# A DeltaNet scan on one core: the triangle's inverse by quarter-array products

## The chip, the core and the metric

The kernel runs on one core of a Trainium2 chip. TensorE multiplies (a 128x128 array), VectorE and ScalarE move and change data between PSUM and SBUF, GpSimd does element work in SBUF, SyncE starts transfers. The metric is device time in microseconds; lower is better.

## The reference, cut to what matters

Two layers of a backbone over 512 latent tokens and 256 context tokens, width 1024. Each layer has two SwiGLU blocks and between them a token mixer of four gated DeltaNet heads and eight RWKV-7 heads, each scanned in both directions. The change is in the DeltaNet part:

```python
a_strict = jnp.where(strict, jnp.einsum('bhnid,bhnjd->bhnij', k, k) * decay * beta[..., :, None], 0.0)
rhs = jnp.concatenate([k * (beta * jnp.exp(gc))[..., None], v * beta[..., None]], axis=-1)
sol = lax.linalg.triangular_solve(a_strict, rhs, left_side=True, lower=True, unit_diagonal=True)
...
v_new = u_n - jnp.einsum('bhcd,bhde->bhce', w_n, s)
o_n = jnp.einsum('bhcd,bhde->bhce', qd_n, s) + jnp.einsum('bhij,bhje->bhie', attn_n, v_new)
s = s * cd_n[..., None, None] + jnp.einsum('bhcd,bhce->bhde', kd_n, v_new)
```

Per chunk and head the unit lower triangle I + A is solved. The kernel uses chunks of 128 tokens, so A is 128x128.

## The kernel before, in words

Each engine runs its own program; semaphores order them. A layer has ten phases with all engines waiting at their ends: feed-forward, projection, DeltaNet scan (`pe_dn`, `act_dn`, `dve_dn`, `pool_dn`), projection, features, RWKV scan (`pe_rw` and its relatives), and output and feed-forward phases.

The DeltaNet scan has 6 steps a layer (2 context chunks, then 4 latent ones), 12 in all. Each step handles 8 triangles: four heads in each of two directions (`g` = 0 and 1). Direction g owns PSUM banks 4g to 4g+3 and its own SBUF tiles, four heads side by side. Every engine goes through the steps in a hardware loop (`Fori`).

A step: TensorE spreads the decays (L1279), multiplies keys by keys and keys by queries (L1283, L1288) and transposes (L1292, L1300). VectorE and ScalarE make the decay matrices, GpSimd weights them (L1248, L1251, L1254), VectorE makes A (L1414) and the first X (L1417, L1419). Then the inverse X of I + A is built by doubling: at level l, diagonal blocks of 2^l are inverted, and each pair is joined through the block below its diagonal. Seven levels, 0 to 6, reach 128. Y is X transposed. A level l > 0 is

- `times_even` (L1169): A's transpose times the even column blocks of X, four products of 64 columns a direction;
- a mask on VectorE (L1427, tile TD);
- `times_packed` (L1174): Y times TD;
- a subtraction into X on VectorE (L1431);
- four transposes of X (L1331), which ScalarE copies to Y (L1389).

All products are float32 with 128x128 weights; the two directions alternate, so that one's products cover the other's VectorE work. Level 0 has only the transposes, followed by keys times state (L1338; VectorE uses it in L1437 and L1441). After level 6, Y multiplies the right side (L1345), and the state and output products follow (L1353, L1356, L1357). A float32 product appears in the trace as two records, a transpose as one.

The RWKV scan inverts its triangles in the same manner with chunks of 64. Two 64x64 triangles lie one above the other in 128 partitions, and each product is issued twice, for partitions 0 to 63 and for 64 to 127 (`times`, L1896; `lower_times_x`, L1988; `x_times_lower`, L2001), with VectorE's L2133 and L2143 and ScalarE's L2071. Its TensorE code is unrolled; VectorE, ScalarE and GpSimd loop. In its start VectorE copies the masks it needs (L2104, L2106).

At the very start GpSimd makes the constant masks, `level` among them (L276 to L286); TensorE waits for them (L295).

Of the kernel before, what the change touches and what calls it, by code (L numbers as in the profile page):

```python
# [7 lines left out]
ALU = mybir.AluOpType  # L8
ACT = mybir.ActivationFunctionType

P = 128
# [24 lines left out]
def build(nc, x, c, ctx, c_ctx, ada_w, ada_b, norm_g, ffn_w13, ffn_w2, w_in, dn_conv, dn_a_log, dn_dt_bias,  # L36
# [3 lines left out]
    with es:  # L40
# [69 lines left out]
        level = sb("level", [P, 7, P])  # L110
# [121 lines left out]
        def pool_setup(pool):  # L232
# [44 lines left out]
            for l in range(7):  # L277
                w = 1 << l
                v = level[:, l, :].rearrange("p (b s j) -> p b s j", s=2, j=w)[:, :, 0, :]
                nb = P // (2 * w)  # L280
                then(g.memset(v, 1.0))

                then(g.affine_select(out=v, in_=v, compare_op=ALU.is_ge, fill=0.0, base=-w,
                                     pattern=[[-2 * w, nb], [0, w]], channel_multiplier=1))

                then(g.affine_select(out=v, in_=v, compare_op=ALU.is_ge, fill=0.0, base=2 * w - 1,  # L286
                                     pattern=[[2 * w, nb], [0, w]], channel_multiplier=-1))
# [857 lines left out]
        EVEN = P // 2  # L1145
# [10 lines left out]
        def packed_bank(b, l):  # L1156
            return packed(PS[:, b, 0:4 * EVEN], l)

        def packed_sbuf(t, l):
            return packed(t.rearrange("p a b -> p (a b)")[:, 0:4 * EVEN], l)  # L1160
# [5 lines left out]
        def times_even(pe, b, lhs, x, l):  # L1166

            for u in range(4):
                mm = pe.matmul(packed_bank(b, l)[:, u], lhs[:, u, :], even(x[:, u, :], l, "p"), start=True, stop=True)  # L1169
            return mm  # L1170

        def times_packed(pe, b, lhs, x):
            for u in range(4):
                mm = pe.matmul(PS[:, b, u * EVEN:(u + 1) * EVEN], lhs[:, u, :],  # L1174
                               x.rearrange("p a b -> p (a b)")[:, u * EVEN:(u + 1) * EVEN], start=True, stop=True)
            return mm

# [3 lines left out]
        XS = 6 * LEVELS_DN + RW_CHUNKS * LEVELS_RW  # L1181
        TS = XS - STEPS
        XTS = XS - RW_CHUNKS
# [19 lines left out]
        kst_ready, s_scaled = dsem("kst_ready"), dsem("s_scaled")  # L1203

# [67 lines left out]
        def pe_dn(pe, layer):  # L1272
            for first, steps, a, w in dn_loops(layer):
                with pe.Fori(0, steps) as i:
# [35 lines left out]
                    for l in range(n):  # L1310
# [14 lines left out]
                        for g in range(2):  # L1325
# [4 lines left out]
                            for u in range(DN_H):  # L1330
                                mm = pe.transpose(PS[:, c, u * P:(u + 1) * P], X[g][:, u, :], ident[:, :])  # L1331
# [1228 lines left out]
```

## Time and profile before

| | us |
|---|---|
| median of 3 runs (4900.68 to 4907.02) | 4905.58 |
| profiled execution | 4901.45 |
| its span | 4899.8 |
| TensorE busy in the span | 4409.8 (90%) |
| VectorE | 1991.6 (41%) |
| ScalarE | 1366.0 (28%) |
| GpSimd | 532.2 (11%) |

The rest of the profiled execution lies around the span. The two DeltaNet scans stand at about 874 to 1202 us and 3406 to 3736 us of the span, the two RWKV scans at about 1494 to 1863 and 4023 to 4391. Busy records of TensorE overlap one another, so the distance from one start to the next says more than a record's length. "PEclk" is the granted clock as a share of 2.4 GHz.

### The profile page before, as it was taken

To read this page: it belongs to the slowest core of one execution; us is meant where nothing else is said; L and a number is where in the kernel's file an instruction comes from. 1 tells how busy PE (TensorE), PEld (TensorE's weight loads), DVE (VectorE), ACT (ScalarE), POOL (GpSimd) and SP (SyncE) were. 2 spreads that over 40 slices of the span, in tenths; PEclk is the share of its full clock that TensorE was granted. 3 is DMA by queue.
4 is the path that set the end of the run, shared out by engine and by line. 5 is a ranking of instruction groups with operands and counts; after the bars stand their busy time and mean duration, and the time that the engine had idled before them with its cause. 6 is when DMAs were issued, how large, how long until landed. Compare 5 with 4: busy or idle time off the path is not lost. (4 is left out here: it accounts for less than half of the span.)

```text
span 4899.8 us, 101076 instructions
## 1 busy us (share of the span) xinstructions
PE 4409.8 (90%) x43461; PEld 3932.3 (80%) x43461; DVE 1991.6 (41%) x2817; ACT 1366.0 (28%) x1958; POOL 532.2 (11%) x690
## 2 busy tenths in 40 slices
PE   6999989898948996999998999988998849996998
PEld 5998977887827995889897999977887629984887
DVE  3222254454475445322223222353444484446334
ACT  3211133232242222321113211243222242223322
POOL 1000000332032110000100000001321051100000
PEclk8999999999959998999999999999999859998999
DMA  5233231000200002233423222121000100012332
GB/s 199 79 111 109 71 112 39 14 1 4 60 7 3 4 4 78 78 124 95 154 77 112 66 62 60 59 62 35 1 0 24 47 1 4 4 42 75 97 94 69
DMA packets 344215, 286.50 MB, mean 58 GB/s; under 512 B 9086, under 2 KB 316772, under 8 KB 343396
## 3 DMA queue, kind: packets, MB, share of 16 engines
q1 hardware_dynamic: 326628, 218.92, 15.0%
q0 software_dynamic: 17280, 62.92, 3.7%
q8 instruction: 262, 4.29, 0.4%
q14 instruction: 45, 0.37, 0.0%
HBM read 270.27 MB, written 11.53 MB: 58 GB/s over the span
## 5 line engine op out<-in xcount | busy, mean ns | idle before, releaser
L646 PE MATMUL PS<-x_hi,w_hi 128*128 128x384 f32 (+1 forms) x2464 | 678.1, 344 | 17.6 <-DVE x_lo L550 16.1
L646 PE MATMUL PS<-x_lo,w_hi 128*128 128x384 f32 (+1 forms) x2464 | 676.3, 344 | 0.0
L646 PE MATMUL PS<-x_hi,w_lo 128*128 128x384 f32 (+1 forms) x2464 | 676.2, 343 | 0.0
L646 PEld LDWEIGHTS PS<-x_hi,w_hi 128*128 128x128 f32 x2464 | 450.3, 189 | 38.7 <-issue 24.4
L646 PEld LDWEIGHTS PS<-x_lo,w_hi 128*128 128x128 f32 x2464 | 450.2, 189 | 13.9
L646 PEld LDWEIGHTS PS<-x_hi,w_lo 128*128 128x128 f32 x2464 | 449.7, 189 | 13.7
L779 DVE TENSOR_TENSOR silu_buf<-silu_buf,PS 128x768 f32<-128x768 f32 (+1 forms) x88 | 78.1, 887 | 786.2 <-ACT silu_buf L712 786.2
L1896 PE MATMUL PS<-arena 64*64 64x64 f32 (+1 forms) x9216 | 356.9, 229 | 12.1 <-POOL arena L1879 5.6
L622 DVE TENSOR_TENSOR w_lo<-raw_w,w_hi 128x2048 fp32r<-128x2048 f32 x136 | 311.7, 2292 | 133.2 <-ACT w_hi L617 133.2
L690 PE MATMUL PS<-hidden_hi,w_hi 128*128 128x256 f32 (+1 forms) x1232 | 346.7, 351 | 19.3 <-DVE hidden_lo L784 19.3
L617 ACT ACTIVATE w_hi<-raw_w 128x2048 fp32r<-128x2048 f32 x136 | 259.5, 1908 | 338.5 <-PE PS L690 331.4
L1896 PEld LDWEIGHTS PS<-arena 64*64 64x64 f32 x9216 | 331.4, 136 | 23.1 <-issue 16.6
L690 PE MATMUL PS<-hidden_lo,w_hi 128*128 128x256 f32 (+1 forms) x1232 | 339.3, 345 | 0.0
L690 PE MATMUL PS<-hidden_hi,w_lo 128*128 128x256 f32 (+1 forms) x1232 | 338.5, 345 | 0.0
L690 PEld LDWEIGHTS PS<-hidden_hi,w_hi 128*128 128x128 f32 x1232 | 227.7, 189 | 75.0 <-issue 25.9
L765 DVE SCALAR_TENSOR_TENSOR arena<-PS,mod,arena 128x512 f32 (+3 forms) x168 | 100.2, 632 | 455.3 <-PE PS L690 455.2
L712 ACT ACTIVATE silu_buf<-PS 128x768 f32<-128x768 f32 (+1 forms) x88 | 66.9, 760 | 778.6 <-PE PS L646 778.5
L690 PEld LDWEIGHTS PS<-hidden_lo,w_hi 128*128 128x128 f32 x1232 | 233.2, 189 | 29.7
L690 PEld LDWEIGHTS PS<-hidden_hi,w_lo 128*128 128x128 f32 x1232 | 233.2, 189 | 29.3
L410 POOL DMA_DIRECT2D arena<-in_ada_w_dram x120 | 86.6, 724 | 1340.6 <-PE PS L419 1105.8
L1389 ACT ACTIVATE arena<-PS 128x512 f32<-128x512 f32 x168 | 100.3, 597 | 317.1 <-PE PS L1331 313.4
L2071 ACT ACTIVATE arena<-PS 128x256 f32<-128x256 f32 x240 | 91.8, 383 | 318.9 <-PE PS L1896 316.9
(341 smaller groups left out, 7803.5 us busy)
## 6 DMA issues: line engine op xcount, KB each, us to landing
raw_w<-in_ffn_w_dram SPq DMA_DIRECT2D x240, 512.0 KB, 4.4
arena<-in_ada_w_dram POOLq DMA_DIRECT2D x120, 512.0 KB, 6.1
arena<-in_w_in_dram SPq DMA_DIRECT2D x64, 512.0 KB, 3.9
arena<-in_ada_w_dram SPq DMA_DIRECT2D x6, 2048.0 KB, 14.6
raw_w<-in_ffn_w_dram SPq DMA_DIRECT2D x32, 384.0 KB, 3.5
arena<-in_w_out_dram SPq DMA_DIRECT2D x16, 512.0 KB, 4.2
h_save<-arena SPq DMA_DIRECT2D x16, 384.0 KB, 2.3
arena<-h_save SPq DMA_DIRECT2D x2, 3072.0 KB, 9.9
```

Of the source, the lines that this page charges most:

```text
L410: pool.dma_start(ada_buf[b], src[:, 2 * b:2 * b + 2, bass.ds((first + 4 * i) * P, 4 * P)]).then_inc(ada_landed[b], 16)
L617: nc.scalar.activation(w_split[HI][:, b, :], raw_w[:, b], ACT.Copy).then_inc(w_high_ready, 1)
L622: nc.vector.tensor_tensor(w_split[LO][:, b, :], raw_w[:, b], w_split[HI][:, b, :].bitcast(F32), ALU.subtract).then_inc(w_low_ready, 1)
L646: mm = pe.matmul(PS[:, 4 * b + 2 * g + s, 0:half], w[wo][:, k, g, :], x_split[xo][:, k, a + s * half:a + (s + 1) * half], start=(k == 0 an ...
L690: mm = pe.matmul(PS[:, 2 * c + s, 0:wd], w[wo][:, f, c * P:(c + 1) * P], hid_split[xo][:, f, a0:a0 + wd], start=(f == 0 and q == 0), stop= ...
L712: nc.scalar.activation(silu_buf[:, b, a:T].rearrange("p (s w) -> p s w", s=pieces), PS[:, 4 * b:4 * b + pieces, 0:half], ACT.Silu).then_in ...
L765: ins = nc.vector.scalar_tensor_tensor(v, PS[:, 2 * c + s, 0:w], g, v, ALU.mult, ALU.add)
L779: nc.vector.tensor_tensor(prod.rearrange("p (s w) -> p s w", s=pieces), prod.rearrange("p (s w) -> p s w", s=pieces), PS[:, 4 * b + 2:4 * ...
L1389: sc.activation(Y[g], bank(4 * g), ACT.Copy).then_inc(y_ready[g], 1)
L1896: mm = pe.matmul(PS[p, bank_, at + u * width:at + (u + 1) * width], lhs(u)[p], rhs(u)[p], start=True, stop=True)
L2071: sc.activation(YR[r][g], half_bank(4 * g + 1), ACT.Copy).then_inc(y_ready[g], 1)
```

## The change

The 128x128 triangle is taken apart as two 64x64 triangles on its diagonal and one 64x64 corner below. Levels 0 to 5 never join anything across the middle, so X, Y and the masked product live in packed tiles (`XP`, `YP`, `TP`): partitions 0 to 63 hold the upper block, 64 to 127 the lower one, 64 columns a head. Each product becomes two, one per half of the partitions; transposes become products with a 64x64 identity (`id_c`). The last copies of Y go into the two diagonal blocks of the full tile, and level 6 is done for the corner alone: A's corner times X's upper block, times minus one (`T6`), times the lower block of Y, copied into Y's upper right block. The lower left block of Y is zeroed once a layer. TensorE's loop over the steps is unrolled. The masks are made for 64 columns in both halves by GpSimd at the start, and the RWKV scan uses them in place of its own copies.

```diff
-        level = sb("level", [P, 7, P])
+        level = sb("level", [P, 6, P // 2])
+        id_c = sb("id_c", [P, P // 2])
+        HALVES = (slice(0, 64), slice(64, 128))
...
+            for p in HALVES:
+                then(g.tensor_copy(id_c[p], ident[p, p]))
+                for l in range(6):
+                    w = 1 << l
+                    v = level[p, l, :].rearrange("p (b s j) -> p b s j", s=2, j=w)[:, :, 0, :]
+                    nb = P // (4 * w)
+                    then(g.memset(v, 1.0))
+
+                    then(g.affine_select(out=v, in_=v, compare_op=ALU.is_ge, fill=0.0, base=-w,
+                                         pattern=[[-2 * w, nb], [0, w]], channel_multiplier=1))
+
+                    then(g.affine_select(out=v, in_=v, compare_op=ALU.is_ge, fill=0.0, base=2 * w - 1,
+                                         pattern=[[2 * w, nb], [0, w]], channel_multiplier=-1))
...
+        XP, T6 = ([X[g].rearrange("p a b -> p (a b)")[:, 256 * n:256 * n + 256].rearrange("p (u t) -> p u t", u=DN_H)
+                   for g in range(2)] for n in range(2))
+        TP = [TD[g].rearrange("p a b -> p (a b)")[:, 0:128].rearrange("p (u t) -> p u t", u=DN_H) for g in range(2)]
+        YP = [TD[g].rearrange("p a b -> p (a b)")[:, 256:512].rearrange("p (u t) -> p u t", u=DN_H) for g in range(2)]
...
+        def blocks(b, p=slice(0, P)):
+            return PS[p, b, 0:256].rearrange("p (u t) -> p u t", u=DN_H)
...
         def pe_dn(pe, layer):
+
+            def times(b, width, lhs, rhs):
+
+                for u in range(DN_H):
+                    for p in HALVES:
+                        mm = pe.matmul(PS[p, b, u * width:(u + 1) * width], lhs(u, p), rhs(u, p), start=True, stop=True)
+                return mm
+
             for first, steps, a, w in dn_loops(layer):
-                with pe.Fori(0, steps) as i:
+                for i in range(steps):
...
-                                times_even(pe, c + 1, AT[g], X[g], l).then_inc(tx_summed[g], 1)
+                                for u in range(DN_H):
+                                    for p in HALVES:
+                                        mm = pe.matmul(packed(PS[p, c + 1, 0:128], l)[:, u], AT[g][p, u, p],
+                                                       even(XP[g][p, u, :], l, "p"), start=True, stop=True)
...
-                                times_packed(pe, c + 2, Y[g], TD[g]).then_inc(xd_summed[g], 1)
+                                times(c + 2, 32, lambda u, p: YP[g][p, u, :], lambda u, p: TP[g][p, u, :]).then_inc(xd_summed[g], 1)
...
-                            for u in range(DN_H):
-                                mm = pe.transpose(PS[:, c, u * P:(u + 1) * P], X[g][:, u, :], ident[:, :])
-                            mm.then_inc(x_turned[g], 1)
+                            times(c, 64, lambda u, p: XP[g][p, u, :], lambda u, p: id_c[p]).then_inc(x_turned[g], 1)
...
+                    lo, hi = HALVES
+                    for g in range(2):
+                        for u in range(DN_H):
+                            mm = pe.matmul(blocks(4 * g + 1, hi)[:, u], AT[g][lo, u, hi], XP[g][lo, u, :], start=True, stop=True)
+                        mm.then_inc(tx_summed[g], 1)
+                    for g in range(2):
+                        pe.wait_ge(tx_masked[g], ts + n)
+                        pe.wait_ge(y_ready[g], yt + n)
+                        for u in range(DN_H):
+                            mm = pe.matmul(blocks(4 * g + 2, lo)[:, u], T6[g][hi, u, :], Y[g][hi, u, hi], start=True, stop=True)
+                        mm.then_inc(xd_summed[g], 1)
                     for g in range(2):
                         c = 4 * g
-                        pe.wait_ge(y_ready[g], XTS * layer + n * (first + i) + n)
+                        pe.wait_ge(y_ready[g], yt + n + 1)
                         pe.wait_ge(r_ready[g], it + 1)
                         for u in range(DN_H):
...
-                            sc.activation(Y[g], bank(4 * g), ACT.Copy).then_inc(y_ready[g], 1)
+                                act.wait_ge(xd_summed[g], TS * layer + n * (first + i) + l)
+                            if l < n - 1:
+                                ins = sc.activation(YP[g], blocks(4 * g), ACT.Copy)
+                            else:
+                                for p in HALVES:
+                                    ins = sc.activation(Y[g][p, :, p], blocks(4 * g, p), ACT.Copy)
+                            ins.then_inc(y_ready[g], 1)
+                    lo, hi = HALVES
+                    for g in range(2):
+                        act.wait_ge(xd_summed[g], TS * layer + n * (first + i) + n)
...
+            for g in range(2):
+                v.memset(Y[g][HALVES[1], :, HALVES[0]], 0.0).then_inc(y_ready[g], 1)
...
-                        v.tensor_tensor(X[g], DM[g], bc(level[:, 0, :], 1, [P, DN_H, P]), ALU.mult).then_inc(x0_step[g], 1)
+                        for p in HALVES:
+                            ins = v.tensor_tensor(XP[g][p], DM[g][p, :, p], bc(level[p, 0, :], 1, [P // 2, DN_H, P // 2]), ALU.mult)
+                        ins.then_inc(x0_step[g], 1)
                         dve.wait_ge(x0_step[g], it + 1)
-                        v.tensor_tensor(X[g], bc(ident[:, :], 1, [P, DN_H, P]), X[g], ALU.subtract).then_inc(x_ready[g], 1)
...
-                            dve.wait_ge(tx_summed[g], TS * layer + (n - 1) * (first + i) + l)
-                            v.tensor_tensor(packed_sbuf(TD[g], l), packed_bank(4 * g + 1, l), level_mask(l), ALU.mult).then_inc(tx_masked[g], 1)
+                            dve.wait_ge(tx_summed[g], TS * layer + n * (first + i) + l)
+                            v.tensor_tensor(TP[g].rearrange("p u (b j) -> p u b j", j=1 << l), packed(PS[:, 4 * g + 1, 0:128], l),
+                                            level_mask(l), ALU.mult).then_inc(tx_masked[g], 1)
                         for g in range(2):
-                            dve.wait_ge(xd_summed[g], TS * layer + (n - 1) * (first + i) + l)
+                            dve.wait_ge(xd_summed[g], TS * layer + n * (first + i) + l)
                             dve.wait_ge(x_turned[g], XTS * layer + n * (first + i) + l)
-                            v.tensor_tensor(even(X[g], l), even(X[g], l), packed_bank(4 * g + 2, l), ALU.subtract).then_inc(x_ready[g], 1)
+                            x = even(XP[g], l)
...
+                    for g in range(2):
+                        hi = HALVES[1]
+                        dve.wait_ge(tx_summed[g], TS * layer + n * (first + i) + n)
+                        v.tensor_scalar(T6[g][hi], blocks(4 * g + 1, hi), -1.0, None, ALU.mult).then_inc(tx_masked[g], 1)
...
-                v.tensor_copy(id_c[p], ident[p, p])
                 v.tensor_copy(ak_mask[p, 0:D], upto_strict[p, p])
-                v.tensor_copy(level_c[p], level[p, 1:LEVELS_RW, p])
```

On TensorE, a level before (in the loop's body, here level 1, the turning after it and the start of level 2):

```order
L1169 MATMUL PS<-arena 128x64 x8
L1320 ISA
L1174 MATMUL PS<-arena 128x64 x8
L1327 REGISTER_ALU
L1331 MATMUL PS<-ident,arena 128x128 x8
L1169 MATMUL PS<-arena 128x64 x8
```

The same place in the unrolled code of after (L1323 is A times X, L1273 the helper `times` for Y times TP and for the turning by `id_c`):

```order
L1323 MATMUL PS<-arena 64x32 x16
L1273 MATMUL PS<-arena 64x32 x16
L1273 MATMUL PS<-id_c,arena 64x64 x16
L1323 MATMUL PS<-arena 64x32 x16
L1273 MATMUL PS<-arena 64x32 x16
```

Each set of 8 whole-array instructions has become 16 on quarters of the array, and the register instructions between them are gone.

TensorE at the end of a step before: level 6, the last turning, and the right side L1345:

```order
L1327 REGISTER_ALU
L1331 MATMUL PS<-ident,arena 128x128 x8
L1169 MATMUL PS<-arena 128x64 x8
L1320 REGISTER_ALU
L1174 MATMUL PS<-arena 128x64 x8
L1327 REGISTER_ALU
L1331 MATMUL PS<-ident,arena 128x128 x8
L1345 MATMUL PS<-arena 128x128 x8
```

After: level 5 with its turning, the corner (L1349 is A times X, L1355 is Y times T6), and the right side L1362:

```order
L1323 MATMUL PS<-arena 64x32 x16
L1273 MATMUL PS<-arena 64x32 x16
L1273 MATMUL PS<-id_c,arena 64x64 x16
L1349 MATMUL PS<-arena 64x64 x8
L1355 MATMUL PS<-arena 64x64 x8
L1362 MATMUL PS<-arena 128x128 x8
```

Of level 6 two sets of 8 quarter products are left, without a turning.

VectorE in the head of a step before, where A (L1414) and the first X (L1417, L1419) are made, direction by direction, then the attention product (L1423) and the first mask:

```order
L1414 TENSOR_TENSOR arena<-arena,PS 128x512
L1417 TENSOR_TENSOR arena<-arena,level 128x512
L1419 TENSOR_TENSOR arena<-ident,arena 128x512
L1414 TENSOR_TENSOR arena<-arena,PS 128x512
L1417 TENSOR_TENSOR arena<-arena,level 128x512
L1419 TENSOR_TENSOR arena<-ident,arena 128x512
L1421 REGISTER_ALU
L1423 TENSOR_TENSOR arena<-arena,PS 128x512 x2
L1426 ISA
L1427 TENSOR_TENSOR arena<-PS,level 128x256 x2
```

After (L1442 is A, L1446 and L1449 the first X, L1453 the attention product, L1457 the mask):

```order
L1442 TENSOR_TENSOR arena<-arena,PS 128x512
L1446 TENSOR_TENSOR arena<-arena,level 64x256 x2
L1449 TENSOR_TENSOR arena<-id_c,arena 128x256
L1442 TENSOR_TENSOR arena<-arena,PS 128x512
L1446 TENSOR_TENSOR arena<-arena,level 64x256 x2
L1449 TENSOR_TENSOR arena<-id_c,arena 128x256
L1451 REGISTER_ALU
L1453 TENSOR_TENSOR arena<-arena,PS 128x512 x2
L1456 ISA
L1457 TENSOR_TENSOR arena<-PS,level 128x128 x2
```

Each direction's X comes from three smaller operations in place of two large ones, in the same place of the order.

## Rows read from the trace of the kernel before

**Rows 1.** The page, part 4: chain by line, share of the span.

```profile
PE PS L646 12%; PE PS L832 7%; PE PS L690 6%; PE PS L1896 3%; PE PS L1174 1%; PE PS L1169 1%; PE PS L2001 1%; PE PS L1988 1%; PE PS L1331 1%; PE PS L1338 0%; DVE arena L2220 0%; DVE arena L1793 0%; PE PS L841 0%; PE PS L853 0%; DVE arena L1431 0%
```

**Rows 2.** Stages; columns: window, us, busy per engine (count), clock, DMA.

```profile
874.00:1184.00 310.00, 279.98 (x2180) 258.88 (x2180) 150.68 (x272) 91.87 (x161) 107.28 (x108) 0.93 0.01 3
...
1494.00:1863.00 369.00, 360.50 (x11136) 354.54 (x11136) 150.27 (x441) 96.40 (x240) 41.43 (x118) 0.99 0.02 4
```

**Rows 3.** Chain, end of one DeltaNet step; columns: start us, us, what, count.

```profile
3503.24 0.43 DVE arena L1431
...
3503.71 0.66 PE PS L1331 x4
3504.37 1.73 PE PS L1169 x16
3506.10 1.80 PE PS L1174 x16
...
3507.93 0.43 DVE arena L1431
...
3508.40 0.66 PE PS L1331 x4
...
3509.10 2.05 PE PS L1345 x16
```

**Rows 4.** Chain, last RWKV level of a chunk, same columns.

```profile
4262.08 0.91 PE PS L1988 x32
4262.99 1.05 PE PS L2001 x32
...
4264.05 1.15 PE PS L1896 x32
```

**Rows 5.** Timeline, head of a step; columns: start, us, engine, line, what, idle before.

```profile
3524.93 0.69 DVE L1417 TENSOR_TENSOR arena<-arena,level 128x512 f32<-128x512 f32 x1
...
3525.50 1.04 POOL L1248 TENSOR_TENSOR arena<-arena 128x512 f32<-128x512 f32 x1 [1.33 <-ACT arena L1376]
3525.65 1.44 DVE L1419 TENSOR_TENSOR arena<-ident,arena 128x512 f32<-128x512 f32 x1
...
3528.07 1.59 POOL L1254 TENSOR_TENSOR arena<-arena,upto_incl 128x512 f32<-128x512 f32 x1
...
3528.58 1.64 DVE L1419 TENSOR_TENSOR arena<-ident,arena 128x512 f32<-128x512 f32 x1
...
3530.27 1.12 PE L1331 MATMUL PS<-ident,arena 128*128 128x128 f32 x4 [1.35 <-DVE arena L1419]
...
3531.18 3.62 PE L1338 MATMUL PS<-arena 128*128 128x128 f32 x16
3531.20 1.27 POOL L1254 TENSOR_TENSOR arena<-arena,upto_incl 128x512 f32<-128x512 f32 x1
```

**Rows 6.** Lines; columns: count, ns min/median/max, first and last start, forms.

```profile
L1427 DVE TENSOR_TENSOR arena<-PS,level x144: 423/424/425, 895.3 to 3723.9; 128x256 f32<-128x256 f32 x144
L2133 DVE TENSOR_TENSOR arena<-PS,arena x240: 275/291/293, 1500.8 to 4384.7; 128x128 f32<-128x128 f32 x120
L2071 ACT ACTIVATE arena<-PS x240: 378/383/385, 1503.8 to 4386.8; 128x256 f32<-128x256 f32 x120
L2106 DVE COPY arena<-level x4: 471/474/477, 1492.7 to 4026.4; 64x320 f32<-64x320 f32 x4
```

**Rows 7.** The same for one line of whole-array products.

```profile
L1356 PE MATMUL PS<-arena x192: 274/275/276, 925.5 to 3733.8; 128*128 128x128 f32 x192
```

**Rows 8.** Stretches in the head of the step, columns as in rows 2.

```profile
3532.00:3534.00 2.00, 2.00 (x12) 2.00 (x11) 0.69 (x1) 0.02 (x1) 2.00 (x3) 0.50 0.00 0
```

**Rows 9.** Timeline of the start, columns as in rows 5.

```profile
16.81 1.04 PE L295 MATMUL PS<-ident,arena 113*128 113x113 f32 x4 [16.81 <-POOLq L288]
...
20.76 8.30 PE L307 MATMUL PS<-ident,arena 128*128 128x128 f32 x48 [2.69 <-DMA arena<-in_x_dram]
...
54.44 3.27 PE L385 MATMUL PS<-arena,cs 128*2 128x512 f32 x16 [2.60 <-DMA arena<-in_ada_w_dram]
```

More of the change, by code:

```diff
@@ L1164, in level_mask @@
             return bc(m, 1, [P, 4, m.shape[1], m.shape[2]])
[L1166 to L1176, printed above, removed]
         STEPS = 6 + RW_CHUNKS
-        XS = 6 * LEVELS_DN + RW_CHUNKS * LEVELS_RW
-        TS = XS - STEPS
-        XTS = XS - RW_CHUNKS
+        XS = 6 * (LEVELS_DN - 1) + RW_CHUNKS * LEVELS_RW
+        TS = XTS = XS - RW_CHUNKS
+        Y_MORE = 7
         def dsem(name):
@@ L1203, in build, with y_count @@
         kst_ready, s_scaled = dsem("kst_ready"), dsem("s_scaled")
+        def y_count(layer, c):
+            return (XTS + Y_MORE) * layer + 1 + LEVELS_DN * c
         def dn_loops(layer):
@@ L1308, in pe_dn @@
                         mm.then_inc(at_turned[g], 1)
-                    n = LEVELS_DN
+                    n = LEVELS_DN - 1
+                    xs, ts, yt = XS * layer + n * (first + i), TS * layer + n * (first + i), y_count(layer, first + i)
                     for l in range(n):
@@ L1364, in act_dn @@
             sc = nc.scalar
[L1365 removed]
+            n = LEVELS_DN - 1
             for first, steps, a, w in dn_loops(layer):
@@ L1387, in act_dn @@
                             if l > 0:
-                                act.wait_ge(xd_summed[g], TS * layer + (n - 1) * (first + i) + l)
-                            sc.activation(Y[g], bank(4 * g), ACT.Copy).then_inc(y_ready[g], 1)
+                                act.wait_ge(xd_summed[g], TS * layer + n * (first + i) + l)
[8 more added lines that the diff above has]
+                        act.wait_ge(xd_summed[g], TS * layer + n * (first + i) + n)
+                        sc.activation(Y[g][lo, :, hi], blocks(4 * g + 2, lo), ACT.Copy).then_inc(y_ready[g], 1)
                     for g in range(2):
@@ L1835, in build @@
         ab_mask, ak_mask = region(26880, 2 * D), region(27008, 2 * D)
-        lower0, lower0_t, id_c = (region(27136 + 64 * n, D) for n in range(3))
-        level_c = region(27328, LEVELS_RW - 1, D)
+        lower0, lower0_t = (region(27136 + 64 * n, D) for n in range(2))
+        level_c = level[:, 1:LEVELS_RW, :]
         y_moved, masks_made = dsem("y_moved"), sem("masks_made")
@@ L1849, in rw_counts @@
             own = RW_CHUNKS * layer + c
-            xs = XS * layer + 6 * LEVELS_DN + LEVELS_RW * c
+            xs = XS * layer + 6 * (LEVELS_DN - 1) + LEVELS_RW * c
             ts = TS * layer + 6 * (LEVELS_DN - 1) + (LEVELS_RW - 1) * c
-            xt = XTS * layer + 6 * LEVELS_DN + (LEVELS_RW - 1) * c
+            xt = ts
             return it, own, xs, ts, xt
@@ L1927, in new_values @@
                         pe.wait_ge(r_ready[g], it + 1)
-                        pe.wait_ge(y_ready[g], xt + n - 1)
+                        pe.wait_ge(y_ready[g], xt + Y_MORE * (layer + 1) + n - 1)
                         times(4 * g + 3, 0, D, lambda u: y[g][:, u, :], lambda u: R_T[g][:, u, :]).then_inc(vn_summed[g], 1)
@@ L1997, in x_times_lower @@
                         else:
-                            pe.wait_ge(y_ready[g], xt2 + l - 1)
+                            pe.wait_ge(y_ready[g], xt2 + Y_MORE * (layer + 1) + l - 1)
                         for u in range(NB):
```

33 lines of the change are left out of this document (10 added, 23 removed).

## The prediction

> **What bounds the kernel now.** The page's chain comes first: TensorE holds it nearly throughout, and the DeltaNet scan (lines 1169 to 1345) has some 3% of the span in it [rows 1]. The change is worth what that scan gives. The stretches come next: in the DeltaNet stretch TensorE is busy 280 of 310 us at a mean clock of 0.93, in the RWKV stretch 360 of 369 us at 0.99, with five times as many instructions [rows 2]. The RWKV scan already inverts its triangle with pairs of 64x64 products, so it is the nearest measured relative of what the DeltaNet scan becomes.
>
> Then the chain inside one level. A level is: turn X (L1331), A times X (L1169), mask on VectorE, Y times that (L1174), subtract on VectorE (L1431). The chain runs 0.43 us of L1431, 0.04 of handing over, 0.66 of turning the second direction, 1.73, 1.80, and again L1431: from 3503.71 to 3508.40 it is 4.69 us a level [rows 3]. Only the subtraction of the second direction shows; the masks (0.42 us, rows 6) and ScalarE's copies of Y lie under the other direction's products. The whole-array products set the pace: 16 records in 1.73 us, 0.108 us a record, for only 64 columns. L1345 with 128 columns takes 2.05 us for its 16, a wait included [rows 3], so fewer columns have bought little here, and what a smaller weight block buys is the question.
>
> In RWKV's last level, which has no other work filled in, the same three sets of 32 records take 0.91 (L1988), 1.05 (L2001) and 1.15 us (L1896), 3.11 together, with masks, subtractions and waits in it [rows 4]. That is 0.028 us a record without a wait.
>
> **The sum, for one of 12 steps** (144 masks in L1427 are 12 steps of 6 levels and 2 directions, rows 6).
>
> Levels 1 to 5. Each now has 16 + 16 products of 32 columns and 16 of 64, 96 records, exactly the counts, tiles and columns of rows 4, and the VectorE operations halve from 128x256 to 128x128, 0.42 to 0.29 us, ScalarE's copy from 128x512 to the 0.38 us of 128x256 [rows 6]. So 3.11 in place of 4.69: 1.58 each, 7.9 us. In level 2 the two 128x512 operations L1437, which stand between subtraction and mask, now outlast the products above them: subtraction ends 0.46 after the last product, two L1437 at 0.64 (0.69 for a 128x512 operation alone, rows 5) take 1.28, so the mask starts at 1.74, while the product it reads ends at 1.49 + 0.2. I lose 0.1.
>
> Last level. Before, from the last product of level 5 to L1345: one whole level 4.69, then 0.03 + 0.43 + 0.04 + 0.66 + 0.04, 5.9 us. After, counted from the first turning product (0.05 after that last product, its X being ready): turning 1.15; corner A times X, 8 records a direction on one quarter of the array. Rows of before have no such run. From below they cannot beat 0.028 a record; from above they cost a whole-array record, 0.108. I take 0.057, since each quarter of a pair gets every second record, so each quarter by itself goes at 0.057. First direction 1.15 to 1.61, second to 2.07. VectorE's T6 (64x256 out of PSUM, priced at the 0.42 of L1427) 1.80 to 2.22 and 2.27 to 2.69. ScalarE's two half copies of Y per direction, 0.38 each, end at 1.4 and 2.2, in time. Corner Y times T6: 2.27 to 2.73, 2.73 to 3.2. ScalarE copies the first corner 2.9 to 3.3. VectorE's L1441, queued behind the second T6, ends at 3.39 (0.69 for 128x512, rows 5) and is later, so L1345 starts at 3.45 + 0.05 = 3.5, 2.4 earlier. Its 2.05 us, in which it waits for ScalarE's second copy, become the 1.78 of 16 records. Together 2.65.
>
> Level 0. X is now made by two 64x256 operations and one 128x256 per direction in place of two of 128x512. Undisturbed that is an estimated 1.1 us (three operations between 0.29 and 0.42) for 1.4, twice. But GpSimd works beside it, and the two engines hold each other up: L1417 takes 0.69 alone, L1419 takes 1.44 and 1.64 when it meets L1248 and L1254, and L1254 takes 1.27 or 1.59 [rows 5]. A shorter operation saves only its own length; three can meet three GpSimd operations where two met two. Ends: if none meets, VectorE is done 1.3 us earlier; if the second half product and the subtraction each wait out a GpSimd operation, 0.7 later. I take 0.2 earlier. The second turning has 16 records at half clock (0.96) for 1.12: another 0.15. The slow clock stays: the engine stands at 0.50 after its idle time before L1331, through L1338 (3.62 us for 16 records) and into level 1 [rows 5, 8]; that loss is in both versions. The attention product waits for L1254 of the second direction, which ends 3532.47 [rows 5]; the first product that needs it comes some 2 us later even after the gain.
>
> Between whole-array and quarter products TensorE may have to run empty. No row shows it; it costs from 0 to what a record is longer than its slot, 0.275 less 0.108 [rows 7], 0.17. Two such places lie on the path (into L1338 and out of it), 0.1 each: 0.2. The Trainium skill ("TensorEngine Tiling (Array Packing)", Key Properties) says that a change of tiling mode drains the engine; the scan would then pay the upper end, 0.15 us a step more, and no run yet shows it.
>
> Sum: 7.9 - 0.1 + 2.65 + 0.2 + 0.15 - 0.2 = 10.6 us a step, 127.2 for 12.
>
> Outside. The RWKV stage loses four small copies on VectorE (two of them 0.47 us, rows 6) once a layer; GpSimd's own copies and TensorE's products beside them leave 0.2 a layer, 0.4 in all (0 to 1.2). Setup grows: GpSimd makes the masks for two halves, 38 small instructions for 21, which I make 4 to 5 us longer; TensorE starts L295 at 16.8 right behind it and would reach L307 some 1.5 us late, since that waited 2.69 for the tokens [rows 9]. Later TensorE waits for weights by DMA again, 2.60 us before L385 at 54.4, which swallows it. Cost 0, at most 1.5. The two memsets of Y lie under VectorE's idle time. The unrolled TensorE code is cheap if code arrives in time: RWKV's is unrolled too and is busy 360 of 369 us [rows 2].
>
> The profiled execution took 4901.45 us (span 4899.8), 4 us under the median 4905.58. 4901.5 - 127.6 = 4773.9; against the median 4778.
>
> **Rivals.** (1) The corner does not overlap. If on one quarter a weight load must wait for the product before it, a record costs up to 0.108 and each of the four corner sets 0.86 in place of 0.46. A times X ends 2.87, Y times T6 of the first direction 3.7, its copy 4.3: L1345 starts 0.8 to 1.2 later, 12 to 15 us in all, about 4792. For it: nothing in the trace has this shape. Against: whole-array records share all rows and still start every 0.108 while each lasts 0.275 with its load beside it [rows 7]. The Trainium skill ("TensorE: Matmul & The Clock Gate", The mechanism) says that weight loads overlap running products only where the row group differs; read strictly it gives this rival, and the whole-array records disagree with the strict reading.
>
> (2) GpSimd takes back more at level 0: 0.7 later in place of 0.2 earlier, 0.9 a step, 11 us: 4789. For it the 1.44 and 1.64 of L1419; against it that the new operations are half as long.
>
> (3) Slower than before: the quarter products do not bring the clock back. Each step begins with the engine at 0.50; if it stayed there, a level would take 96 records at 0.057, 5.5 us, 2.4 more than forecast, 12 for five levels, the corner 2 more, and the 64 records from L1345 on, 7 us now, some 6.5 more: 20 us a step against a gain of 10.6, so 10 us a step slower, 5020 to 5030. It decides from half of that work at half clock on. Against it: RWKV's stretch of the same products is at 0.99. For it: only that DeltaNet's steps have an idle time each, which RWKV's have not.
>
> (4) The head gets off lightly: the operations miss GpSimd's, or the clock does not fall since the idle time shrinks: 13 to 20 us better, 4762.
>
> (5) It does not do what it says: code for the unrolled loop arrives late, or quarter pairs do not run side by side. Rows 2 and 4 speak against both.
>
> **Numbers.** Forecast 0.62; rival 1 0.13; rival 2 0.11; rival 4 0.09; rival 3 0.03; rival 5 0.02, near no change or a little slower. Time 4778. Range 4757 to 4806: the low end is the head without GpSimd and free switches of tiling (15 us), with 6 for the forecast's own slack; the high end rivals 1 and 2 together. A measurement of this kernel tells 0.2% (10 us) from no change; faster 0.95, within it 0.01, slower 0.04.
>
> **What would show it.** Levels 2 to 5 at 3.1 us and 0.03 us a record (if 4 or more, the pairs or the hand-overs fail); L1437 the only late VectorE operation; the corner's records 0.057 or 0.108 apart; L1441 or the corner copy releasing the product behind it; the two VectorE operations that make X under L1248, L1251 and L1254; the clock at 0.50 for one stretch a step and 1.00 from level 2 on. I am wrong if the step shrinks by under 8.5 or over 12.5 us, or if something outside the scan moves by more than 3 us.

## The result and the profile after

| | before | after |
|---|---|---|
| median | 4904.1 of 4 runs (4900.68 to 4907.02) | 4781.1 of 4 runs (4776.6 to 4782.66) |
| profiled execution, span | 4901.45, 4899.8 | 4781.18, 4779.5 |
| TensorE busy | 4409.8 | 4290.5 |
| instructions in the trace | 101076 | 107933 |

The ratio is 0.9748 [0.9731, 0.9765]: 2.5% faster, 123 us. The forecast was 4778.

The same stretches as in [rows 2] (DeltaNet, then RWKV; columns as there):

```profile
873.00:1142.00 269.00, 235.70 (x4104) 218.03 (x4104) 140.19 (x284) 83.61 (x181) 102.73 (x108) 0.91 0.02 5
1434.00:1800.00 366.00, 358.33 (x11129) 354.06 (x11131) 149.20 (x438) 95.60 (x239) 42.00 (x119) 0.99 0.02 4
```

From its first product to its last a DeltaNet scan takes 268.3 and 268.1 us in place of 326.8 and 327.0. So 117 of the span's 120 us are in the two scans. Inside them, as the mean of the ten steps that follow another one (worked out from the records; a step is counted from the previous one's last scaling of the state):

| piece of a step | before | after | change | forecast |
|---|---|---|---|---|
| head: until the second direction's first X is made | 13.62 | 14.36 | +0.74 | -0.2 |
| turning, keys times state, to level 1 | 4.36 | 4.81 | +0.45 | +0.05 |
| levels 1 to 5 | 23.92 | 15.49 | -8.43 | -7.8 |
| corner in place of level 6, then right side, state and outputs | 12.40 | 9.73 | -2.67 | -2.65 |
| step | 54.31 | 44.40 | -9.91 | -10.6 |

The levels first. Level 1 begins at the half clock and takes 3.37 us in the mean, 5.16 before; levels 2 to 5 take 3.03 each, 4.69 before. The chain of waits of after, over two of them (columns as in [rows 3]):

```profile
3376.31 2.12 PE PS L1273 x64
3378.43 0.91 PE PS L1323 x32
3379.34 1.95 PE PS L1273 x58
```

A level is 0.91 of A times X (L1323) and 2.12 of Y times TP and the turning (both L1273): 3.03 us in place of 4.69, and VectorE's subtraction, which stood in the chain before with 0.43 [rows 3], is no longer in it.

The starts of the records say where the time went (medians at the full clock). A whole-array record starts 0.112 us after the one ahead of it. The quarter records start in pairs, one per half of the partitions and 0.007 apart, and a pair follows a pair every 0.058. A level was 40 records and is now 48 pairs, 48 times 0.058 or 2.8 us. Some waiting is left: the set after A times X starts 0.146 us behind its last record and the turning 0.143 behind the set before it, where a set that waits for nothing (A times X after the turning) follows after 0.052. These are the first mask and the first subtraction, 0.09 each.

The timeline of the last level (start, us, engine, line, what, idle before):

```profile
3379.97 0.29 DVE L1463 TENSOR_TENSOR arena<-arena,PS 128x128 f32<-128x128 f32 x1 [0.29 <-PE PS L1273]
...
3381.04 1.56 ACT L1410 ACTIVATE arena<-PS 64x256 f32<-64x256 f32 x4 [2.18 <-PE PS L1273]
...
3381.30 0.92 PE L1349 MATMUL PS<-arena 64*64 64x64 f32 x13
3381.79 0.89 DVE L1473 TENSOR_SCALAR arena<-PS 64x256 f32<-64x256 f32 x2 [1.06 <-PE PS L1349]
...
3382.27 1.14 PE L1355 MATMUL PS<-arena 64*64 64x64 f32 x16
3382.71 1.29 DVE L1477 TENSOR_TENSOR arena<-arena 128x512 f32<-128x512 f32 x2
3382.98 0.85 ACT L1415 ACTIVATE arena<-PS 64x256 f32<-64x256 f32 x2 [0.38 <-PE PS L1355]
...
3383.55 2.02 PE L1362 MATMUL PS<-arena 128*128 128x128 f32 x16
```

The corner's 16 records of one set start 0.058 us apart (median), each 0.22 long or more, so they overlap. L1362 starts when the first copy of the corner (L1415) and the first right side (VectorE's L1477, queued behind both T6, L1473) are there.

The head of the step, with before's in [rows 5]:

```profile
3398.59 0.67 DVE L1442 TENSOR_TENSOR arena<-arena,PS 128x512 f32<-128x512 f32 x1
...
3399.30 0.85 DVE L1446 TENSOR_TENSOR arena<-arena,level 64x256 f32<-64x256 f32 x2
...
3399.95 1.10 POOL L1243 TENSOR_TENSOR arena<-arena 128x512 f32<-128x512 f32 x1 [1.57 <-ACT arena L1393]
3400.18 1.14 DVE L1449 TENSOR_TENSOR arena<-id_c,arena 128x256 f32<-128x256 f32 x1
...
3401.01 1.23 POOL L1246 TENSOR_TENSOR arena<-arena 128x512 f32<-128x512 f32 x1
3401.25 0.67 DVE L1442 TENSOR_TENSOR arena<-arena,PS 128x512 f32<-128x512 f32 x1
3401.96 1.97 DVE L1446 TENSOR_TENSOR arena<-arena,level 64x256 f32<-64x256 f32 x2
...
3402.31 1.33 POOL L1249 TENSOR_TENSOR arena<-arena,upto_incl 128x512 f32<-128x512 f32 x1
...
3403.61 1.23 POOL L1246 TENSOR_TENSOR arena<-arena 128x512 f32<-128x512 f32 x1
3403.96 1.15 DVE L1449 TENSOR_TENSOR arena<-id_c,arena 128x256 f32<-128x256 f32 x1
...
3405.17 1.12 PE L1273 MATMUL PS<-id_c,arena 64*64 64x64 f32 x16 [1.92 <-DVE arena L1449]
3406.22 3.78 PE L1344 MATMUL PS<-arena 128*128 128x128 f32 x16
```

For the first direction the two L1446 take 0.85 together; for the second, beside GpSimd's L1246 and L1249, 1.97, and L1449 1.15. TensorE's wait before the second turning is 1.92 us, where before it was 1.35 [rows 5]. By line (count, ns min/median/max):

```profile
L1446 DVE TENSOR_TENSOR arena<-arena,level x48: 416/549/1403, 883.7 to 3580.2; 64x256 f32<-64x256 f32 x48
```

The same instruction takes 416 or 1403 ns. A long one ends 0.28 us after the GpSimd operation that it met (the median of 14 records of L1446 and of 24 of L1449); before, L1417 and L1419 ended 0.55 after it. The granted clock behind the wait (window, us, busy, clock, DMA; before's is [rows 8]):

```profile
3404.00:3406.00 2.00, 0.83 (x16) 0.55 0.00 0
3406.00:3408.00 2.00, 2.00 (x14) 0.50 0.01 4
```

It stays at 0.50, which is 1.2 GHz, through keys times state (L1344) and is back at 1.00 before level 2.

Setup grew by less than forecast: the first product behind GpSimd's masks starts at 19.90 in place of 16.81 (3.1 later; 4 to 5 were forecast), the tokens' product at 21.09 in place of 20.76 [rows 9] (0.33; some 1.5 were forecast).

```profile
19.90 1.04 PE L299 MATMUL PS<-ident,arena 113*128 113x113 f32 x4 [19.90 <-POOLq L292]
...
21.09 4.18 PE L311 MATMUL PS<-ident,arena 128*128 128x128 f32 x19
```

Of those 0.33 us nothing is left at the start of the first scan, which comes at 873.5 us against 874.8.

### The profile page after: what moved, and what is told of

It reads as the page before. It is cut to its first block and busy times, and to the rows that moved or that the text cites. A ratio compares the mean times of both kernels' runs of the same rounds, so it can differ in the third digit from the quotient of the medians.

```text
span 4779.5 us, 107933 instructions
## 1 busy us (share of the span) xinstructions
PE 4290.5 (90%) x47013; PEld 3819.6 (80%) x47013; DVE 1958.3 (41%) x2813; ACT 1339.5 (28%) x1982; POOL 526.5 (11%) x707
## 5 line engine op out<-in xcount | busy, mean ns | idle before, releaser
L1931 PE MATMUL PS<-id_c,arena 64*64 64x64 f32 x6144 | 212.4, 219 | 0.0
L1931 PEld LDWEIGHTS PS<-id_c,arena 64*64 64x64 f32 x6144 | 196.3, 135 | 1.6
L1931 PE MATMUL PS<-arena 64*64 64x128 f32 (+1 forms) x3072 | 153.0, 248 | 11.6 <-POOL arena L1914 5.4
```

Source lines behind the costliest of these rows:

```text
L1931: mm = pe.matmul(PS[p, bank_, at + u * width:at + (u + 1) * width], lhs(u)[p], rhs(u)[p], start=True, stop=True)
```

## The experiments

A label's time is one run where no interval is given; the median of before on the same chip stands beside it. "Theory" and "rival" are the ones of each expectation.

**unrolled_alone**: the kernel before, with only TensorE's loop over the steps unrolled.

```diff
-                with pe.Fori(0, steps) as i:
+                for i in range(steps):
```

> The kernel before with TensorE's loop over the steps unrolled and nothing else. Theory: levels stay at 4.69 us and the time within 5 us of 4904. Rival (register instructions between the sets cost part of each level): levels shorter by 0.1 us or more, 10 us or more in all.

4904.43 us (before 4907.8), levels 2 to 6 at 4.69, as expected; a step takes 54.46 in place of 54.31. The unrolling is worth nothing that shows; the gain is the blocks'.

**corner_alone**: whole-array levels 0 to 5, the corner for level 6, TensorE unrolled.

```diff
-                    for l in range(n):
+                    for l in range(n - 1):
...
+                        for u in range(DN_H):
+                            mm = pe.matmul(quarter(4 * g + 1, hi)[:, u], AT[g][lo, u, hi], X[g][lo, u, lo], start=True, stop=True)
...
+                            mm = pe.matmul(quarter(4 * g + 2, lo)[:, u], T6[g][hi, u, :], Y[g][hi, u, hi], start=True, stop=True)
```

> The kernel before with one part of the change alone: level 6 by its corner (two sets of 8 quarter products, T6, one corner copy, no last turning), and TensorE's loop unrolled. Levels 0 to 5 stay on the whole array. Theory: the stretch from the level 5 product to the right side's product falls from 9.58 us by 2.3 to 2.7, the rest of the step stays, about 29 us in all, some 4875 us. Rival (the last level gained in the changed kernel only because X and Y were already small): under 1.5 us a step, above 4886 us.

4877.39 us (before 4907.8). From level 5's start to the right side 9.58 became 7.26: -2.32 us, against -2.64 in the full change, whose last turning is by quarters too. The levels stay at 4.69. So the corner is about a quarter of the gain: 2.32 times 12 is 28 us of 123. The 30.4 us of the run are no clean measure of it. The step shrank by 3.17, because the clock also came back earlier than in the trace of before (the piece up to level 1 took 3.89 in place of 4.36, level 1 itself 4.69 in place of 5.16), and stages that the edit doesn't touch took back 8 us.

**half_major**: the changed kernel, with the halves one after the other inside each set in place of alternating.

```diff
-                for u in range(DN_H):
-                    for p in HALVES:
+                for p in HALVES:
+                    for u in range(DN_H):
```

> The changed kernel with each set of 16 quarter products issued as 8 of the upper half and then 8 of the lower half, in place of alternating. Same products, same VectorE and ScalarE work. Theory (the level is shorter because alternate quarters run side by side): a record costs 0.057 us as in the corner, a set of 32 records 1.8 us in place of 0.93, a level about 5.5 us in place of 3.03, the step 12 us longer, some 4925 us, slower than before the change. Rival (the gain comes from fewer columns and the halved VectorE and ScalarE operations): a level stays at 3.0 to 3.3 us, 4780 to 4800 us.

4828.3 us (before 4907.8). Neither number came. Two sets of a level and the start of the next, on TensorE's timeline:

```profile
3406.81 1.23 PE L1323 MATMUL PS<-arena 64*64 64x32 f32 x29
3407.91 1.43 PE L1273 MATMUL PS<-arena 64*64 64x32 f32 x32
3409.20 1.36 PE L1273 MATMUL PS<-id_c,arena 64*64 64x64 f32 x29
```

A level takes 3.73 us, where alternating gives 3.03 and whole-array products gave 4.69. My theory had the pace of one quarter right: the last records of each set of A times X, all on one quarter and of 32 columns, start 0.058 us apart (median), like the corner's of 64 columns. What failed is that the edit did not keep the halves from overlapping. A run of eight records on one half begins 0.26 to 0.29 us after the run ahead of it on the other, while a run takes 0.41 from its first start to its last, so the two quarters still overlap for much of the time. So this run shows what the order is worth, 0.70 us a level, and not what a level without any overlap would take; 96 records at 0.058 would be an estimated 5.6 us, more than the 4.69 of before.

**gpsimd_held**: the changed kernel, with GpSimd's work on the keys held back until the second first X is made.

```diff
+                pool.wait_ge(x_ready[1], XS * layer + (LEVELS_DN - 1) * (first + i) + 1)
                 for g in range(2):
                     pool.wait_ge(ktok_moved[g], it + 1)
```

> The changed kernel; GpSimd waits until both directions' first X is made before it starts on the key and attention factors (L1246, L1249). Theory (the first X is late because each VectorE operation in SBUF waits out a GpSimd operation): the 64x256 operations of the second direction fall to about 0.42 us each and the 128x256 one too, the first product on X starts 1.3 to 1.6 us earlier in each step; the attention product comes later but is not yet needed: 14 to 18 us less, some 4765 us. Rival (operations on 64 partitions are slow by themselves): their durations stay at 0.55 and 1.15 us and the time stays or grows, by up to 1 us a step if the attention product is now late.

4765.44 us (before 4907.8), 15.7 less than after, as the theory expected. The second direction's three operations:

```profile
3392.93 0.68 DVE L1443 TENSOR_TENSOR arena<-arena,PS 128x512 f32<-128x512 f32 x1
3393.64 0.85 DVE L1447 TENSOR_TENSOR arena<-arena,level 64x256 f32<-64x256 f32 x2
...
3394.52 0.42 DVE L1450 TENSOR_TENSOR arena<-id_c,arena 128x256 f32<-128x256 f32 x1
...
3395.03 1.05 POOL L1247 TENSOR_TENSOR arena<-arena 128x512 f32<-128x512 f32 x1 [2.31 <-DVE arena L1450]
```

1.97 became 0.85 and 1.15 became 0.42; the piece from the second A to the second X went from 3.88 to 2.02. The two scans together are 20.8 us shorter (257.9 and 257.7); the stages around them took 5 back, with shifts of up to 3.5 us either way in stages that the edit leaves alone (one RWKV scan took 370.1). In the first step of each scan the clock now falls over the levels: level 1 takes 5.23 and 5.28, level 2 takes 5.12.

**before_held**: the same hold in the kernel before.

```diff
+                pool.wait_ge(x_ready[1], XS * layer + LEVELS_DN * (first + i) + 1)
```

> The kernel before, with the same hold on GpSimd as in gpsimd_held: in each step its multiplication of the keys by the decay (and what follows on it) waits until VectorE has made the second first X. Asked is whether the 0.68 us that the changed kernel loses between the start of the second A and the end of the second first X (3.88 against 3.20) is GpSimd's doing, or the length of the three new operations themselves. Theory: it is GpSimd's. Without it the changed kernel needs 2.02 us (measured); the kernel before should need about 2.15 (three operations of 128x512 at 0.69 and hand-overs), so not less than the changed one. Step shorter by 0.7 to 1.0, time 4892 to 4896. Rival: the new operations are not shorter than the old ones, many small ones cost their fixed part; then the kernel before, held, is under 1.6 us here and stays well ahead of the changed one.

4887.06 us (before 4896.77).

```profile
3518.08 0.67 DVE L1415 TENSOR_TENSOR arena<-arena,PS 128x512 f32<-128x512 f32 x1
3518.79 0.69 DVE L1418 TENSOR_TENSOR arena<-arena,level 128x512 f32<-128x512 f32 x1
...
3519.52 0.69 DVE L1420 TENSOR_TENSOR arena<-ident,arena 128x512 f32<-128x512 f32 x1
```

Here the piece goes from 3.20 to 2.13 us, which is the theory's 2.15; the rival wanted less than 1.6. The step shrinks by 1.22, somewhat over the 0.7 to 1.0 expected. Undisturbed, the changed kernel is 0.11 us ahead (2.02); beside GpSimd it is 0.68 behind. GpSimd costs 1.07 us before and 1.86 after: all of the loss in this piece is GpSimd's.

**ks_early**: the changed kernel, with keys times state (L1344) ahead of level 0's turning, in TensorE's wait for the first X.

```diff
+                    for g in range(2):
+                        pe.wait_ge(s_updated[g], it + 2 * layer + 1)
+                        pe.wait_ge(at_moved[g], it + 1)
+                        for u in range(DN_H):
+                            mm = pe.matmul(PS[:, 4 * g + 3, u * P:(u + 1) * P], KTc[g][:, u, :], S[g][:, u, :], start=True, stop=True)
+                        mm.then_inc(ks_ready[g], 1)
                     n = LEVELS_DN - 1
```

> The changed kernel with keys times state (L1344, 16 whole-array records) issued in front of the level 0 turning, where TensorE waits for the first X anyway. Two places where the path goes from quarter to whole-array products and back fall away, and the half-clock stretch has less to slow. Theory (these products and the 0.45 us that the two places seem to cost stand on the path, 1.11 + 3.71 us from the second turning to level 1): that stretch falls to 1.0 to 1.3 us; then the attention product (GpSimd's L1249, VectorE's L1453) is what level 1 waits for, so 3 to 4.2 us a step are left, 36 to 50 us in all, about 4738 us. Rival (level 1 cannot start before the attention product, which is hardly later than now): under 1 us a step, above 4769 us.

4738.75 us (4 runs, 4737.2 to 4740.27), ratio to before 0.9662 [0.9646, 0.9678]: 42 us less than after, inside the 36 to 50 expected, and the fastest here. A step is 41.06 us.

The first step of a scan:

```profile
3338.81 2.07 PE L1316 MATMUL PS<-arena 128*128 128x128 f32 x16
...
3342.61 0.69 DVE L1452 TENSOR_TENSOR arena<-arena,PS 128x512 f32<-128x512 f32 x1 [0.56 <-POOL arena L1249]
3343.21 0.48 DVE L1456 TENSOR_TENSOR arena<-PS,level 128x128 f32<-128x128 f32 x2
3343.55 1.12 PE L1273 MATMUL PS<-arena 64*64 64x32 f32 x32 [0.46 <-DVE arena L1456]
```

Keys times state (L1316) runs at the full clock, 2.07 us for 3.78, and ends before the second X is made. The next thing late is the mask of level 1 (L1456), queued behind the attention product, which waits for GpSimd: 0.46 us. That is the theory's picture, but it holds only in the first step of each scan. The other ten look like this:

```profile
3379.29 2.89 PE L1316 MATMUL PS<-arena 128*128 128x128 f32 x16
3382.11 1.15 PE L1273 MATMUL PS<-id_c,arena 64*64 64x64 f32 x32
3383.09 1.07 PE L1329 MATMUL PS<-arena 64*64 64x32 f32 x32
```

Here the granted clock still falls to 0.50 over keys times state, which takes 2.89 to 3.62 us and ends 0.5 to 1.2 us after the second X. It is what the turning and level 1 wait for; level 1 then takes 3.03 and does not wait for the attention product. From the second X to level 1 it is 1.8 us in the mean, where 1.0 to 1.3 were expected.

**before_ks_early**: the same move in the kernel before, TensorE unrolled. Its edit is the one above, on L1338.

> The kernel before, TensorE unrolled, with keys times state (L1338) moved ahead of level 0's turning, as in ks_early. Asked is how much of the 3.5 us a step that ks_early gained over the changed kernel has to do with the change, and how much any version of this scan would gain. Theory: the product fills TensorE's wait for the first X, which both kernels have (1.35 us before L1331 in the trace of before, 1.92 in the changed one). The kernel before gains that wait less hand-overs and the half clock it leaves, 2.5 to 3.5 us a step, time 4862 to 4875. Rival: the gain is the quarter products' (the two tile changes around keys times state that lay on the path, and a larger wait): then the kernel before gains under 1.5 us a step and takes over 4886.

4873.62 us (before 4896.77), step 51.16 in place of 54.31 (54.46 where TensorE is unrolled). So nearly all of the 3.34 us that ks_early gains a step any version of this scan had to give. Here keys times state takes 2.07 us in all twelve steps: the clock, low only at the start of each scan, no longer falls in any step, which it still does in ten of ks_early. The two scans are 36 us shorter than in the trace of before; the run's time shows 23 of it, since stages that the edit doesn't touch took 8 more than in that trace (one RWKV scan 371.9 for 367.8) and this chip's run of before was the fastest of all. With the product moved in both, the change is worth 10.1 us a step.

**ks_early_held**: both edits.

> Both edits: keys times state early, and GpSimd held until both first X are made. Theory (after the first edit the attention product bounds level 1, so holding GpSimd delays the bound): slower than keys times state early alone, by 0.5 to 1.7 us a step, 4745 to 4760 us. Rival (the gains add): 1.5 to 2 us a step faster than it, some 4718 us.

4795.37 us (4 runs, 4792.52 to 4803.24), ratio 0.9782 [0.9766, 0.9799]. Slower than ks_early, as expected, but by 57 us and not 6 to 20; a step is 46.14 us.

```profile
3372.45 1.12 PE L1274 MATMUL PS<-arena 64*64 64x32 f32 x32 [2.53 <-DVE arena L1457]
3373.49 1.21 PE L1274 MATMUL PS<-id_c,arena 64*64 64x64 f32 x32
3374.49 1.87 PE L1330 MATMUL PS<-arena 64*64 64x32 f32 x32
3376.16 1.90 PE L1274 MATMUL PS<-arena 64*64 64x32 f32 x32
3377.87 1.96 PE L1274 MATMUL PS<-id_c,arena 64*64 64x64 f32 x32
```

The wait grew to 2.53 us, which is the expected part. What I had missed is what comes behind it: the same trace's clock (columns as above)

```profile
3370.00:3372.00 2.00, 0.00 (x0) 1.00 0.00 0
...
3374.00:3376.00 2.00, 2.00 (x53) 0.61 0.01 4
3376.00:3378.00 2.00, 2.00 (x42) 0.50 0.04 8
```

falls to 0.50 after the engine stood empty, and now it stands over the levels: level 2 takes 5.12 us in place of 3.03 in ten of the twelve steps, and level 3 in five.

**one_whole_added**: the changed kernel with one whole-array product put between the two 32-column sets of levels 3, 4 and 5.

```diff
+                            if l >= 3:
+                                pe.matmul(PS[:, 3, 384:448], ident[:, :], ident[:, 0:64], start=True, stop=True)
```

> The changed kernel with one whole-array product (128x128 weights, 64 columns, result unused) added in each of levels 3, 4 and 5 between the set A times X and the set Y times TP, 36 places. Theory (going from quarters to the whole array and back costs 0.1 to 0.3 us each way beside the product's own 0.22): a level with it is 0.45 to 0.75 us longer, 3.5 to 3.8 us. Rival (no cost in the change of tile): 0.22 us longer or less, 3.2 us.

4796.78 us (before 4905.38).

```profile
3381.40 1.07 PE L1323 MATMUL PS<-arena 64*64 64x32 f32 x32
3382.40 0.43 PE L1327 MATMUL PS<-ident 128*128 128x64 f32 x2
3382.77 1.12 PE L1273 MATMUL PS<-arena 64*64 64x32 f32 x32
```

The level with it takes 3.40 us for 3.03, between the theory's 3.5 and the rival's 3.2. From the last quarter record to the next one it is 0.514 us, where quarter sets that wait for nothing follow after 0.052. The two added records account for 0.224 of that at their own pace of 0.112, so the two changes between whole and quarter cost 0.24 together, some 0.12 each. Only 0.37 of it shows, because 0.09 of the place was TensorE's wait for the mask. In one step the clock stayed down over levels 1 and 2 (5.18 and 5.12, step 51.20), some 6 us; in the others it came back sooner than in after.

**one_quarter_added**: the control, a 64x64 product in the same places.

```diff
+                                pe.matmul(PS[0:64, 3, 384:448], ident[0:64, 0:64], ident[0:64, 0:64], start=True, stop=True)
```

> The control of the run before: one 64x64 product of 64 columns added at the same 36 places. Every theory: its own 0.06 to 0.12 us and no more, levels of 3.1 us.

4774.69 us (before 4905.38), levels 3.03, where 0.06 to 0.12 more were expected. The two added records went into the 0.09 of waiting for the mask: from the last record of A times X to the next set it is 0.154 us in place of 0.146. So the control shows that the 0.37 above is the whole array's doing, not what a quarter product costs.

## Why the prediction was right, and where it was not

The time was right (4778 for 4781.1), and the step shrank by 9.91 us where 10.6 was forecast. Of the step's terms the corner hit; the levels gave more than forecast, the head and the turning less.

*Levels.* Right in kind and 0.63 us a step too small. RWKV's last level (3.11) was the right relative. Levels 2 to 5 run at 3.03, 0.08 better each; the 0.1 us put on level 2 for L1437 (now L1469) did not come, since level 2 takes 3.03 in all twelve steps; and level 1, part of it at the half clock, shrank by 1.79 for 1.58. The prediction gave the gain to the pairs [rows 4], and the records bear it out: from record to record on the same part of the array it is 0.058 for the smaller blocks, 0.112 for the whole array, and the pairs make up for having twice the products. The whole-array pace of 0.108 in the sum was 1.73 over 16 records; from start to start it is 0.112.

*Corner.* Right: 2.67 for 2.65, and the pace of a lone quarter 0.058 for 0.057. Rival 1 wanted 0.108 and is out. In this kernel loads and products of one quarter do overlap. A rule of the Trainium skill ("TensorE: Matmul & The Clock Gate", The mechanism) lets weight loads overlap running products only where the row group differs, though the same section also names a background weight buffer as a way out; by the rule alone the corner's records, 0.22 us long with a load beside each, could not start every 0.058, and the trace decides against the rule read so.

*Head.* Here the step of the prediction failed: "I take 0.2 earlier" came out 0.74 later, which is rival 2's mechanism and its size (+0.7). The bound was right and my choice inside it was wrong: I argued that half as long operations give back half as much. But each of the three can be met by a GpSimd operation, and then ends 0.28 us behind that one, nearly whatever its own length. before_held and gpsimd_held show it: the undisturbed lengths differ by 0.11 us only, the disturbance by 0.79. A row that tells which operations are concerned is L1442, which reads PSUM and stays at 0.67 beside GpSimd, while L1446 and L1449, with both inputs in SBUF, do not. They are not the only ones: L1438, a VectorE operation with one input, and that in SBUF, takes 1.26 us for 0.42 beside L1243 in 3 of its 24 records. The Trainium skill ("SBUF — State Buffer", SBUF: two separate sides) says the same: a VectorE operation with two SBUF inputs and a GpSimd one that reads SBUF hold a shared port pair in turn, each for its whole instruction. Weighed in the prediction, it would have spoken for rival 2.

*Turning, keys times state.* +0.45 for +0.05. Priced were a gain of 0.15 for the second turning at half clock and a loss of 0.2 for two tile changes. The 0.15 came from setting 16 records at their pace (0.96) against 1.12, which is the length of L1331's record to its end; from its start to that of L1338 it is 0.91 [rows 5]. The like of it after is 1.05 (3405.17 to 3406.22), and from keys times state to level 1 it is 3.71 for 3.41. The records show where the 0.44 lies, at the half clock: the first record of L1344 starts 0.241 us behind the last pair, where pairs follow after 0.10; its second 0.372 behind the first, where the others follow after 0.213; and L1323 starts 0.351 behind the last one, again for 0.213. That is 0.14, 0.16 and 0.14, all of it at the two tile changes, so the turning itself gained nothing and the two changes cost 0.44, not 0.2. At the full clock a change costs some 0.12 (one_whole_added), near the 0.1 taken; at the half clock it is some 0.22. The Trainium skill ("TensorEngine Tiling (Array Packing)", Key Properties) says that changing the tiling mode drains the engine, and one_whole_added against one_quarter_added agrees; it gives no price. The 0.17 that I had as the upper end holds at the full clock only.

*Clock.* As said: 0.50 once a step, 1.00 from level 2 on; rival 3 is out. Yet ks_early_held, two steps of gpsimd_held and one of one_whole_added (levels 5.18 and 5.12, step 51.20) show its mechanism at work where the clock falls just ahead of the levels or over them.

*Outside.* Setup 0, as forecast, though by smaller delays than the sum had [rows 9]. The two RWKV scans became 1.8 and 1.2 us shorter (367.8 to 366.0 and 366.6) for 0.2 each forecast. That is more than noise: the gain comes evenly, a chunk starting 30.29 or 30.20 us after the one ahead of it where before it was 30.46 or 30.38. In the five traces with the old masks no RWKV scan takes less than 367.7; in the seven with the new ones 13 of 14 scans take 365.9 to 367.4, and one 370.1. So the four copies, a matter of the scan's start, are not what was gained; no run here shows what is.

So the total was right partly by luck: +1.34 us a step of head and turning that I did not forecast, against 0.65 of levels and corner, and 3 us in the RWKV scans for 0.4.

## What to carry to other kernels

When a triangle's inverse by doubling is bound by TensorE, split it at 64: two 64x64 triangles as alternating quarter products and a corner took 1.66 us from each level and 2.6 from the last. Count VectorE operations in SBUF that stand beside GpSimd by their number, not by their length. And look for independent products that can stand in TensorE's wait: moving one block was worth another 42 us here and 36 us in the scans of the kernel before. But a wait pushed in front of fast products can cost more than itself, since the clock falls behind it.

## What the hardware showed that was not expected

- Products on one quarter start every 0.058 us, with 64 columns (the corner) or 32 (half_major); the other quarter's start 0.007 beside them in the alternating sets, at no cost. A whole-array record of 64 or 128 columns needs 0.112. At the half clock it is 0.107 a pair and 0.213.
- A VectorE operation of 0.42 us lasts up to 1.40 beside GpSimd's, and ends 0.28 after it.
- A change between whole-array and quarter products costs about 0.12 us at the full clock and 0.22 at the half, and nothing that shows was lost by unrolling 12 steps of TensorE code.
- Where the half clock stands over quarter products, a level takes 5.12 us in place of 3.03, or 0.053 us a record in place of 0.032.
